# Split weights at multiples of 256 bytes, the tokens' operands 128 bytes past one

## The chip, the cores and the metric

One core of one Trainium2 chip. The metric is the device time of the whole program in microseconds: 781.03 us, the median of 3 runs (780.86, 781.03, 783.62).

## The reference, cut to what matters

One encoder layer over 512 tokens (two sequences of 256) with a model width of 1024, all in float32: an embedding LayerNorm, a token mixer, and a mixture of 16 experts of which each token takes two.

```python
z = x @ w_in + b_in                       # 1024 -> 3584: attention q, k, v; gating u, v; conv a, g
a  = neighbourhood_attention(q, k, v, rpb) @ w_a_o
bb = (gelu(u) * (W_s layer_norm(gelu(v)) + b_s)) @ w_b_o
c  = silu(layer_norm(depthwise_conv31(glu))) @ w_c_o
g  = sigmoid(x @ w_gate + b_gate)         # three gates of width 1024
m  = (g0 * a + g1 * bb + g2 * c) @ w_o + b_o
x  = layer_norm(ALPHA * x + m)
for e in range(16):                       # grouped top-2 routing
    h = silu(x @ w_e1[e]) * (x @ w_e3[e])
    y = y + gates[:, e:e + 1] * (h @ w_e2[e])
x  = layer_norm(ALPHA * x + y)
```

## The kernel before, in words

Every large product is made of float32 operands that are split in two: `hi`, the value rounded to the matmul's float32r type, and `lo`, what is left. A product is then three matmuls into one PSUM bank, hi x hi, hi x lo and lo x hi (`three`, L1841 to L1845). Each of them is one 128x128 weight load and one stream of 512 columns.

The weights come in units of 128 x 1024 float32 numbers (512 KB). SyncE's queue loads a unit into a ring of raw tiles (`raw`, in the expert stage `raw_more`, `raw_late` and `raw_rows` as well). ScalarE casts it into a slot of `w_hi` (L720), VectorE subtracts and writes a slot of `w_lo` (`cast_lo`, L1052 to L1057), and TensorE waits for `lo_cast` before it takes the unit. `w_hi` and `w_lo` have three slots of 4096 bytes per partition (`SPLIT = 3`); in the expert stage there are four (`M_SPLIT = 4`), and the fourth is in the tiles `w_hi_more` and `w_lo_more`. A slot is free again when the matmuls of its unit are done (`unit_used`).

There are two ways to use a unit. In `features` the split weights are loaded and the tokens' operands (`xT_hi`, `xT_lo`, `branch..`) stream past: so the input projections that are wanted by channel, the gates and the branch outputs. In `tokens` the tokens' operands (`xT`, `mT`, `xgT`, `hT`) are loaded and the weights stream: so v and the gating's v, the output projection and all of the experts. The profile names the operands of a matmul as moving,loaded: `bank<-xT_hi,w_hi` streams xT_hi past a load of w_hi.

The order of work is written out by hand for each engine: 28 units of input projection with attention, gating and convolution in between, 36 units of gates and branches, 8 of the output projection, the router, then 16 experts of 12 units each. For an expert the tokens' rows are gathered by an indirect DMA into `xg` (two buffers), turned by eight transposes (`turn_xg`, L2138), split into `xgT`, and multiplied; the results are scaled and scattered, and the last two experts' results are placed by matmuls with a one-hot operand (`place`, L2229 and L2230: `turned` is loaded, `placed_hi` and `placed_lo` stream) on top of an identity matmul of the running rows (L2239).

SBUF tiles are laid one behind the other in the order in which they are declared; a tile starts at the next multiple of its `line` (32 bytes, or `LINE` = 128 where that is given), and a stack that is closed gives its bytes to the tiles declared after it. The first tile, `raw`, starts at byte 16,512 of each partition. By summing the sizes: `w_hi` starts at 41,088, `w_lo` at 53,376, `const` at 65,664, `vec` at 68,192, `xT_hi` at 69,504, `mT_hi` at 152,448, `w_hi_more` at 155,520, `w_lo_more` at 159,616, `xg` at 163,712, `xgT_hi` at 171,904, `hT_hi` at 192,384. Of these `vec` is 96 bytes past a multiple of 256, and all the others are 128 bytes past one; `onehot` is at 151,040, a multiple of 256. `between` is a tile of 128 bytes that nothing reads or writes. All slots, chunks and column blocks of these operands lie at steps of 512 bytes or a multiple of that.

Of the kernel before, what the change touches and what calls it, by code (L numbers as in the profile page):

```python
# [19 lines left out]
F32R = mybir.dt.float32r  # L20
# [5 lines left out]
D = 1024  # L26
# [27 lines left out]
SPLIT = 3  # L54
M_SPLIT = 4
M_AHEAD = M_SPLIT - 1
LINE = 128
UNIT = 1024
# [10 lines left out]
V_LN1G, V_LN1B, V_ALL = 80, 88, 96  # L69
# [92 lines left out]
def encoder_layer(nc, A, out_prompt, out_sample):  # L162
    banks = plan_banks()
    ctx = ExitStack()
# [14 lines left out]
    def sb(stack, name, shape, dt=F32, line=32):  # L179
        return stack.enter_context(nc.sbuf_tensor(name, [P] + shape, dt, align_bytes=line))  # L180

    raw = sb(ctx, "raw", [RAW, UNIT])
    w_hi = sb(ctx, "w_hi", [SPLIT, UNIT], F32R)
    w_lo = sb(ctx, "w_lo", [SPLIT, UNIT], F32R)
    const = sb(ctx, "const", [C_ALL])
    vec = sb(ctx, "vec", [V_ALL])
    conv_col = sb(ctx, "conv_col", [TAPS, WC])
    stats = sb(ctx, "stats", [TT, 2, 6])
    mv = sb(ctx, "mv", [TT, 2])
# [75 lines left out]
    moe = ExitStack()  # L265
# [30 lines left out]
    gates = sb(moe, "gates", [TT, EXPERTS])  # L296
    most = sb(moe, "most", [1])
    between = sb(moe, "between", [LINE // 4])
    onehot = sb(moe, "onehot", [2, TT, SLOTS], F32R, LINE)
    joint = sb(moe, "joint", [TT, 4])  # L300
    slot_gate = sb(moe, "slot_gate", [2])
# [2 lines left out]
    list_gate = sb(moe, "list_gate", [EXPERTS])  # L304
    list_none = sb(moe, "list_none", [2, 4])
    list_base = sb(moe, "list_base", [2, 4])
    w_hi_more = sb(moe, "w_hi_more", [M_SPLIT - SPLIT, UNIT], F32R, LINE)
    w_lo_more = sb(moe, "w_lo_more", [M_SPLIT - SPLIT, UNIT], F32R, LINE)
    over_xg = ExitStack()
    xg_0 = sb(over_xg, "xg_0", [D])  # L310
    y_last_hi = sb(over_xg, "y_last_hi", [D], F32R)
    over_xg.close()
    xg = sb(moe, "xg", [2, D])
    xgT_hi = sb(moe, "xgT_hi", [2, DC, SLOTS], F32R, LINE)
# [2000 lines left out]
```

## Time and profile before

| | |
|---|---|
| median of 3 runs | 781.03 us |
| span of the profiled execution, first to last instruction | 779.0 us |
| its own time beside the span | not on the page |
| PE (matmul) busy | 747.3 us, 96% of the span, 3516 instructions |
| PEld (weight load) busy | 618.2 us, 79% |
| DVE (VectorE) busy | 609.4 us, 78% |
| ACT (ScalarE) busy | 432.6 us, 56% |
| POOL busy | 72.1 us, 9% |
| mean granted TensorE clock | 0.987 |
| DMA | 175.51 MB, mean 225 GB/s |

How to read it: PE and PEld are two views of TensorE. The duration of a matmul in the lines runs from its start to its modelled end, and matmuls overlap in the pipeline, so what a matmul takes from the span is the step from its start to the start of the next one, which the timeline shows. A row that ends in x2 or x8 merges so many instructions.

### The profile page before, as it was taken

The page shows a single profiled execution, that of the slowest core. Times are in us where ns is not written, and L with a number is a line of the kernel's source. Part 1 is how long each engine was busy: PE and PEld are TensorE (multiplying, and loading weights), DVE is VectorE, ACT ScalarE, POOL GpSimd, SP SyncE. Part 2 cuts the span into 40 slices and gives each one's busy share as a digit, 9 for nine tenths or more (in the row PEclk, how much of TensorE's full clock was granted, in tenths as well). Part 3 has the DMA queues.
Part 4 walks back from the last instruction along what each step waited for, and adds up shares of the span by engine and source line. Part 5 has one row for each costly group of instructions (what it writes and reads, how often), then busy time and mean ns, then how long its engine had stood idle before and what let it go on. Part 6 is the DMA issues. An engine that isn't in the chain of part 4 may idle for free.

```text
span 779.0 us, 10638 instructions
## 1 busy us (share of the span) xinstructions
PE 747.3 (96%) x3516; PEld 618.2 (79%) x3516; DVE 609.4 (78%) x827; ACT 432.6 (56%) x585; POOL 72.1 (9%) x96
## 2 busy tenths in 40 slices
PE   4999999999999999999999979999999999999995
PEld 3888877887888888888888857888888888888873
DVE  5799977776668866535357888999999999999977
ACT  5522134658322244623332366888888888888861
POOL 5000000000000000000011111111111111110314
PEclk9999999999999999999999989999999999999998
DMA  9734657232344352333379587999999999999882
GB/s 294 238 96 101 203 148 209 59 108 82 109 119 124 109 162 82 109 101 89 106 257 343 189 296 234 353 382 384 386 373 386 386 390 368 373 377 367 236 176 111
DMA packets 137488, 175.51 MB, mean 225 GB/s; under 512 B 15418, under 2 KB 75558, under 8 KB 137430
## 3 DMA queue, kind: packets, MB, share of 16 engines
q1 hardware_dynamic: 128896, 154.95, 59.3%
q0 software_dynamic: 7616, 19.34, 8.4%
q10 hardware_dynamic: 934, 0.69, 0.3%
q8 instruction: 23, 0.38, 0.2%
q14 instruction: 19, 0.16, 0.1%
HBM read 164.06 MB, written 19.11 MB: 235 GB/s over the span
## 4 chain that ended last, share of the span: by engine, by line
PE 85%; DVE 7%; DMA 3%; ACT 2%; SPq 2%; issue 1%; POOL 0%; DVEq 0%; ACTq 0%; POOLq 0%
PE bank L1843 25%; PE bank L1844 25%; PE bank L1845 25%; DMA raw<-in_w_in_dram 2%; PE bank L2138 2%; SPq L607 2%; DVE w_lo L1056 1%; DVE conv L1126 1%; PE bank L2059 1%; PE bank L1838 1%; PE bank L2153 1%; PE bank L2239 1%; DVE conv_odd L1126 1%; PE bank L1889 1%; PE bank L1905 1%
## 5 line engine op out<-in xcount | busy, mean ns | idle before, releaser
L1056 DVE TENSOR_TENSOR w_lo<-raw,w_hi 128x1024 fp32r<-128x1024 f32 x103 | 125.0, 1220 | 79.0 <-ACT w_hi L720 78.8
L720 ACT CAST w_hi<-raw 128x1024 fp32r<-128x1024 f32 x103 | 107.1, 1049 | 103.2 <-PE bank L1845 98.4
L1843 PE MATMUL bank<-xT_hi,w_hi 128*128 128x512 f32 x352 | 139.6, 397 | 2.9 <-DVE xT_lo L1094 1.8
L1844 PE MATMUL bank<-xT_lo,w_hi 128*128 128x512 f32 x352 | 138.2, 392 | 0.0
L1845 PE MATMUL bank<-xT_hi,w_lo 128*128 128x512 f32 x352 | 138.1, 392 | 0.0
L1843 PE MATMUL bank<-w_hi,xgT_hi 128*128 128x512 f32 x198 | 80.1, 404 | 1.0 <-issue 1.0
L1843 PEld LDWEIGHTS bank<-xT_hi,w_hi 128*128 128x128 f32 x352 | 66.8, 190 | 17.1 <-issue 3.5
L1845 PEld LDWEIGHTS bank<-xT_hi,w_lo 128*128 128x128 f32 x352 | 66.8, 190 | 14.3
L1844 PEld LDWEIGHTS bank<-xT_lo,w_hi 128*128 128x128 f32 x352 | 66.9, 190 | 13.5
L1845 PE MATMUL bank<-w_hi,xgT_lo 128*128 128x512 f32 x198 | 77.5, 391 | 0.0
L1844 PE MATMUL bank<-w_lo,xgT_hi 128*128 128x512 f32 x198 | 77.3, 390 | 0.0
L835 ACT ACTIVATE gate<-bank,vec 128x512 f32<-128x512 f32 x24 | 16.5, 688 | 83.2 <-PE bank L1845 83.2
L1056 DVE TENSOR_TENSOR w_lo<-raw_more,w_hi 128x1024 fp32r<-128x1024 f32 x40 | 48.2, 1221 | 5.7 <-ACT w_hi L720 5.4
L1056 DVE TENSOR_TENSOR w_lo<-raw_late,w_hi 128x1024 fp32r<-128x1024 f32 x40 | 48.2, 1221 | 4.0 <-ACT w_hi L720 3.9
L1126 DVE SCALAR_TENSOR_TENSOR conv<-conv_in,conv_col,conv 128x512 f32<-128x512 f32 x60 | 44.6, 744 | 0.0
L720 ACT CAST w_hi<-raw_more 128x1024 fp32r<-128x1024 f32 x40 | 41.2, 1049 | 4.5 <-PE bank L1845 4.5
L1845 PEld LDWEIGHTS bank<-w_hi,xgT_lo 128*128 128x128 f32 x198 | 37.2, 188 | 7.9
L1843 PEld LDWEIGHTS bank<-w_hi,xgT_hi 128*128 128x128 f32 x198 | 37.3, 188 | 7.8 <-issue 1.2
L720 ACT CAST w_hi<-raw_late 128x1024 fp32r<-128x1024 f32 x40 | 41.2, 1051 | 2.4 <-PE bank L1845 2.4
L1844 PEld LDWEIGHTS bank<-w_lo,xgT_hi 128*128 128x128 f32 x198 | 37.3, 188 | 6.6
L1126 DVE SCALAR_TENSOR_TENSOR conv_odd<-conv_in,conv_col,conv_odd 128x512 f32<-128x512 f32 x56 | 41.6, 743 | 0.0
L1056 DVE TENSOR_TENSOR w_lo<-raw_rows,w_hi 128x1024 fp32r<-128x1024 f32 x32 | 38.3, 1218 | 0.0
(289 smaller groups left out, 1529.3 us busy)
## 6 DMA issues: line engine op xcount, KB each, us to landing
raw_more<-in_w_e_dram SPq DMA_DIRECT2D x48, 512.0 KB, 8.4
raw<-in_w_e_dram SPq DMA_DIRECT2D x48, 512.0 KB, 9.0
raw_late<-in_w_e_dram SPq DMA_DIRECT2D x48, 512.0 KB, 8.4
raw_rows<-in_w_e_dram SPq DMA_DIRECT2D x48, 512.0 KB, 9.5
raw<-in_w_in_dram SPq DMA_DIRECT2D x28, 512.0 KB, 6.6
raw<-in_w_gate_dram SPq DMA_DIRECT2D x24, 512.0 KB, 3.7
y_scratch<-zeros SPq DMA_DIRECT2D x8, 512.0 KB, 5.1
raw<-in_w_o_dram SPq DMA_DIRECT2D x8, 512.0 KB, 3.7
```

Source lines behind the costliest of these rows:

```text
L607: sp.dma_start(v_win[:, seq, j, :], v_grid[:, WINDOW[j]:WINDOW[j] + KCOLS, :]).then_inc(v_windows, 16)
L720: act.copy(hi_slot(j), raw_slot(j)).then_inc(hi_cast, 1)
L835: act.activation(gate[:, n if n < 2 else r % 2, d, :], bank(name)[:], ACT.Sigmoid, bias=column(V_GATE + n * DC + 2 * r + d)).then_inc(free ...
L1056: dve.tensor_tensor(lo_slot(j), raw_slot(j), hi_slot(j).bitcast(F32), ALU.subtract).then_inc(lo_cast, 1)
L1126: o = dve.scalar_tensor_tensor(out=sum_, in0=shifted, scalar=conv_col[:, k, c:c + 1], in1=sum_, op0=ALU.mult, op1=ALU.add)
L1838: o = pe.transpose(bank(name)[:, k * P:(k + 1) * P], tile(k), ident)
L1843: pe.matmul(out, hi_l, hi_r, start=start, stop=False)
L1844: pe.matmul(out, hi_l, lo_r, start=False, stop=False)
L1845: return pe.matmul(out, lo_l, hi_r, start=False, stop=stop)
L1889: o = pe.matmul(bank(("attended", g))[:, j * P:(j + 1) * P], v_win[:, seq, j, hp * P:(hp + 1) * P], probsT[:, j * P:(j + 1) * P], start=Tr ...
L1905: o = pe.transpose(bank(name)[:, tokens_of(t)], x_in[:, t, c * P:(c + 1) * P], ident)
L2138: o = pe.transpose(psum[M_XT + half][:, k * P:(k + 1) * P], xg[:, q, c * P:(c + 1) * P], ident)
```

## The change

Three tiles are declared elsewhere and one gets a line. `vec` (384 bytes) is declared ahead of `w_hi` rather than behind `const`. So `w_hi` starts at 41,472 and `w_lo` at 53,760, both multiples of 256, and `const` at 66,048, a multiple of 256 as well; `conv_col` and everything behind it up to the expert stage keep their bytes. `w_hi_more` and `w_lo_more` are declared behind `between` rather than behind `list_base`: they start at 151,040 and 155,136, multiples of 256. `onehot` and the lists move up by 8,192 bytes. `xg` starts at 163,680, 96 past a multiple of 256, and `y_last_hi`, which shares its bytes, asks for a line of 128 and keeps its place at 167,808. `xgT` and all behind it keep their bytes. No instruction, wait or DMA is added, removed or put elsewhere.

```diff
@@ -180,10 +180,10 @@
         return stack.enter_context(nc.sbuf_tensor(name, [P] + shape, dt, align_bytes=line))
 
     raw = sb(ctx, "raw", [RAW, UNIT])
+    vec = sb(ctx, "vec", [V_ALL])
     w_hi = sb(ctx, "w_hi", [SPLIT, UNIT], F32R)
     w_lo = sb(ctx, "w_lo", [SPLIT, UNIT], F32R)
     const = sb(ctx, "const", [C_ALL])
-    vec = sb(ctx, "vec", [V_ALL])
     conv_col = sb(ctx, "conv_col", [TAPS, WC])
     stats = sb(ctx, "stats", [TT, 2, 6])
     mv = sb(ctx, "mv", [TT, 2])
@@ -296,6 +296,8 @@
     gates = sb(moe, "gates", [TT, EXPERTS])
     most = sb(moe, "most", [1])
     between = sb(moe, "between", [LINE // 4])
+    w_hi_more = sb(moe, "w_hi_more", [M_SPLIT - SPLIT, UNIT], F32R, LINE)
+    w_lo_more = sb(moe, "w_lo_more", [M_SPLIT - SPLIT, UNIT], F32R, LINE)
     onehot = sb(moe, "onehot", [2, TT, SLOTS], F32R, LINE)
     joint = sb(moe, "joint", [TT, 4])
     slot_gate = sb(moe, "slot_gate", [2])
@@ -304,11 +306,9 @@
     list_gate = sb(moe, "list_gate", [EXPERTS])
     list_none = sb(moe, "list_none", [2, 4])
     list_base = sb(moe, "list_base", [2, 4])
-    w_hi_more = sb(moe, "w_hi_more", [M_SPLIT - SPLIT, UNIT], F32R, LINE)
-    w_lo_more = sb(moe, "w_lo_more", [M_SPLIT - SPLIT, UNIT], F32R, LINE)
     over_xg = ExitStack()
     xg_0 = sb(over_xg, "xg_0", [D])
-    y_last_hi = sb(over_xg, "y_last_hi", [D], F32R)
+    y_last_hi = sb(over_xg, "y_last_hi", [D], F32R, LINE)
     over_xg.close()
     xg = sb(moe, "xg", [2, D])
     xgT_hi = sb(moe, "xgT_hi", [2, DC, SLOTS], F32R, LINE)
```

## Rows read from the trace of the kernel before

**Rows 1.** The page's chain that ended last: by engine, then by line.

```profile
PE 85%; DVE 7%; DMA 3%; ACT 2%; SPq 2%; issue 1%; POOL 0%; DVEq 0%; ACTq 0%; POOLq 0%
PE bank L1843 25%; PE bank L1844 25%; PE bank L1845 25%; DMA raw<-in_w_in_dram 2%; PE bank L2138 2%; SPq L607 2%; DVE w_lo L1056 1%; DVE conv L1126 1%; PE bank L2059 1%; PE bank L1838 1%; PE bank L2153 1%; PE bank L2239 1%; DVE conv_odd L1126 1%; PE bank L1889 1%; PE bank L1905 1%
```

**Rows 2.** Busy time by stretch: PE, PEld, DVE, ACT, POOL, clock, DMA share, GB/s.

```profile
300.00:430.00 130.00, 130.00 (x576) 107.57 (x575) 71.28 (x81) 45.12 (x55) 6.21 (x11) 1.00 0.48 157
...
480.00:750.00 270.00, 270.00 (x1286) 224.94 (x1285) 253.23 (x264) 231.43 (x274) 36.30 (x38) 1.00 1.01 359
```

**Rows 3.** Groups by line and shape, whole span: moving,loaded operand; busy us, mean ns.

```profile
L1844 PE MATMUL bank<-xT_lo,w_hi 128*128 128x512 f32 x352 | 138.2, 392 | 0.0
...
L1844 PE MATMUL bank<-w_lo,xgT_hi 128*128 128x512 f32 x198 | 77.3, 390 | 0.0
...
L1844 PE MATMUL bank<-branch_lo,w_hi 128*128 128x512 f32 x96 | 37.4, 389 | 0.0
...
L1844 PE MATMUL bank<-w_lo,hT_hi 128*128 128x512 f32 x90 | 35.0, 389 | 0.0
...
L1844 PE MATMUL bank<-w_lo_more,xgT_hi 128*128 128x512 f32 x66 | 25.7, 389 | 0.0
...
L1844 PE MATMUL bank<-w_lo,mT_hi 128*128 128x512 f32 x64 | 24.9, 389 | 0.0
...
L1844 PE MATMUL bank<-w_lo,xT_hi 128*128 128x512 f32 x64 | 24.9, 389 | 0.0
...
L1844 PE MATMUL bank<-w_lo_more,hT_hi 128*128 128x512 f32 x30 | 11.7, 389 | 0.0
```

**Rows 4.** Timeline of PE, mixer, weights loaded: start us, us, form.

```profile
319.79 0.39 PE L1844 MATMUL bank<-xT_lo,w_hi 128*128 128x512 f32 x1
...
323.87 0.39 PE L1844 MATMUL bank<-xT_lo,w_hi 128*128 128x512 f32 x1
```

**Rows 5.** Timeline of PE, mixer, weights streaming.

```profile
99.66 0.39 PE L1845 MATMUL bank<-w_hi,xT_lo 128*128 128x512 f32 x1
...
103.97 0.39 PE L1843 MATMUL bank<-w_hi,xT_hi 128*128 128x512 f32 x1
```

**Rows 6.** Groups by line and shape: the identity matmuls of the last sum.

```profile
L2239 PE MATMUL bank<-x,const 128*128 128x512 f32 x16 | 8.2, 591 | 0.0
```

**Rows 7.** Timeline of PE in the last sum.

```profile
758.20 0.39 PE L2230 MATMUL bank<-y_next_lo,next_turned 128*128 128x512 f32 x1
758.43 0.39 PE L2229 MATMUL bank<-y_last_hi,onehot 128*128 128x512 f32 x1
...
759.35 1.02 PE L2239 MATMUL bank<-x,const 128*128 128x512 f32 x2
```

**Rows 8.** Timeline of PE behind two f32 matmuls.

```profile
278.72 0.40 PE L1844 MATMUL bank<-branch_lo,w_hi 128*128 128x512 f32 x1
...
280.57 0.39 PE L1843 MATMUL bank<-branch_hi,w_hi 128*128 128x512 f32 x1
...
281.93 0.39 PE L1843 MATMUL bank<-branch_hi,w_hi 128*128 128x512 f32 x1
```

**Rows 9.** Groups by line and shape: three kinds of transposes.

```profile
L2138 PE MATMUL bank<-const,xg 128*128 128x128 f32 x128 | 16.6, 272 | 0.0
...
L2200 PE MATMUL bank<-const,onehot 128*128 128x128 f32 x8 | 1.2, 272 | 0.0
...
L1838 PE MATMUL bank<-const,w_s_in 128*128 128x128 f32 x4 | 0.6, 272 | 0.0
```

**Rows 10.** Groups by line and shape, 505 to 680 us: the casts on VectorE.

```profile
L1056 DVE TENSOR_TENSOR w_lo<-raw_rows,w_hi 128x1024 fp32r<-128x1024 f32 x20 | 24.0, 1218 | 0.0
...
L1056 DVE TENSOR_TENSOR w_lo_more<-raw,w_hi_more 128x1024 fp32r<-128x1024 f32 x10 | 12.4, 1239 | 1.4 <-ACT w_hi_more L720 1.4
```

**Rows 11.** Chain of waits, 64 to 125 us: start us, us, what.

```profile
68.55 1.13 DVE w_lo L1056
...
106.71 14.31 DMA raw<-in_w_in_dram
```

## The prediction

> **What bounds the kernel now.** I read the chain that ended last first. TensorE holds 85% of it, and the three matmul lines of the split product, L1843 to L1845, hold 25% of the span each [rows 1]. Then the stretches: in the dense part of the mixer (300 to 430 us) and in the expert stage (480 to 750 us) PE is busy for the whole stretch at a granted clock of 1.00, that is 2.4 GHz [rows 2]. In the expert stage VectorE is close behind, 253.23 us busy of 270.00, so 16.8 us are free there, and the DMA share reads 1.01. Nothing but the time from one matmul to the next can move this kernel much, so the question is what a start address does to that time.
>
> How many of these matmuls there are: the eight forms of L1844 count 352 + 198 + 96 + 90 + 66 + 64 + 64 + 30 = 960 [rows 3], and each belongs to a set of three, so 2,880 matmuls of 512 columns, each with a weight load of its own. In 448 of the 960 sets the split weights are loaded and the tokens stream past (the first operand named streams: xT and branch rows); in 512 sets the tokens are loaded and the weights stream (mT, xgT and hT rows, and xT with 64).
>
> Their pace: in a run with weights loaded, 18 steps take 323.87 - 319.79 = 4.08 us, 0.2267 us each [rows 4]; in a run with weights streaming, 19 steps take 103.97 - 99.66 = 4.31 us, 0.2268 us each [rows 5]. The durations of about 390 ns in the lines are pipelined and don't count; the steps do. 2,880 x 0.2267 = 653 us of the 779.0 us.
>
> **The change part by part.** No instruction, wait, semaphore, DMA or queue position is added, removed or moved. Only addresses change. Summing the declared sizes from the first tile's byte 16,512 (64 x 256 + 128): before, all four split weight tiles, xT, the branches, mT, xgT and hT start 128 bytes past a multiple of 256. After, vec's 384 bytes stand ahead of w_hi, so w_hi and w_lo start at 41,472 and 53,760, multiples of 256; the extra slots of the expert stage, w_hi_more and w_lo_more, move to 151,040 and 155,136, multiples of 256 too. The tokens' operands keep their bytes. Side effects: const moves from 128 past to a multiple of 256, onehot by 8,192 bytes, and xg from 128 past to 96 past a multiple of 256.
>
> *Term 1, the 2,880 steps.* Steps between a load and a stream that both sit 128 past are those of rows 4 and 5: 0.2267 us. Is there anything to win or lose in them? The identity matmul of L2239 streams 512 columns in plain f32: two of them take 1.02 us together and one alone about 0.59, so the second starts 0.43 us after the first; that is two passes of 512 columns, 0.214 us a pass, with a load beside it [rows 6 and 7]. A split step is longer by about 0.0127 us. So something of a load beside a full-rate stream costs 12.7 ns, and an address might matter to it. That is the most that can be won.
>
> The trace also has the pair that the change makes: in L2229 and L2230 y_last (128 past) streams while onehot (a multiple of 256) is loaded. From 758.20 to 759.35 there are five steps in 1.15 us, 0.230 us each [rows 7]. So weights loaded from a multiple of 256 against a stream 128 past give no shorter step; they are 3.3 ns longer than the steady pace. But this is just behind f32 matmuls, and there the all-128 pair is slow too: after the f32 matmuls at 278 us, eight steps take 280.57 - 278.72 = 1.85 us, 0.231 us each, and only then do six steps take 281.93 - 280.57 = 1.36 us, 0.2267 us each [rows 8]. Five steps are too few to see where the other pair would settle. The bounds of term 1 are therefore -12.7 ns and +3.3 ns a step, and I take 0: the row nearest in kind (0.230) is no slower than its own transient would be with the old offsets (0.231), and a pace that settles at the same 0.2267 for loaded and for streamed weights, and for slots 0 to 2 and slot 3 alike, doesn't look as if it hung on one distance between addresses.
>
> The Trainium skill (TensorE: Matmul & The Clock Gate, Step-by-step: what each phase is for) says that TensorE has two independent read ports, one for the streaming operand and one for the weight load. By that rule the distance between the two addresses is worth nothing and the time stays; the 12.7 ns over an f32 pass speak against so clean a picture, so I give "no change" no more than half.
>
> *Term 2, the transposes.* xg is loaded for 128 transposes. Transposes that load from 64 past (w_s_in), from 128 past (xg) and from a multiple of 256 (onehot) read 272 ns each [rows 9]. For 96 past there is no row; I take 0, and a nanosecond either way would be 0.13 us. The gather into xg is also at another offset now, but PE has no idle time in 480 to 750 us [rows 2], so it has cover; if that were gone, its delay would stop PE once per expert.
>
> *Term 3, the casts.* VectorE reads raw and w_hi and writes w_lo. Over the existing placements one cast takes from 1218 to 1239 ns [rows 10]. Were all at the long end, an expert's 12 casts would take 12 x 0.021 = 0.25 us more, and the VectorE has about 1.1 us free in each expert (16.8 us over some 15). It is hidden; only a cast of over 1.3 us would show. ScalarE's cast goes with it. vec and const as small operands: nothing.
>
> Sum: 0 + 0 + 0 on a span of 779.0 us. The page shows no total for the profiled execution; the runs' median is 781.03, so some 2.0 us lie around the span, and I forecast 781.0.
>
> **The rivals.**
> *A, slower: the new distance breaks the settled pace.* In place of 0.2267 the steps stay at the 0.230 that the onehot pair shows. Between about 64 and 122 us the mixer waits for conv work, casts and loads rather than for PE [rows 11], some 58 / 0.2267 = 256 steps, so 2,624 steps count: 2,624 x 3.3 ns = 8.7 us, 789.7. If it holds only where weights are loaded (1,344 steps), 1,344 x 3.3 = 4.4 us, 785.4. For it: the five steps of rows 7, which come four times, once for each token tile of the last sum. Against it: they follow f32 matmuls. It decides, with its sign, from 1.5 ns a step (3.9 us over 2,624 steps).
> *B, faster in part: the load and the stream stop meeting in some places.* A step shorter by the same 3.3 ns would give 781.0 - 8.7 = 772.3. For it: a part of the 12.7 ns need not be fixed. Against it: the new pair's mean in rows 7 is not below 0.2267.
> *C, faster in full: the whole 12.7 ns go.* 2,624 x 12.7 ns = 33 us, 748. In the expert stage 384 sets, 1,152 steps, would win 14.6 us, just within VectorE's free 16.8 us, so the casts would become the bound there, with the DMAs beside them. Against it: rows 7 again, plainly, though only for loaded weights; a stream from a multiple of 256 against a load 128 past has no row. The Trainium skill (TensorE: Matmul & The Clock Gate, Back-to-back issue gap) gives N/2.4 + 2.5 ns for a matmul alone, 216 ns at 512 columns; by that the gain would be 10.9 ns a step, an estimate of some 29 us.
> *D, the change does not do what it says:* the loads only sweep the same places in another order, which is the forecast itself.
>
> **How the numbers follow.** No change 0.49, A 0.29, B 0.14, C 0.08. The likeliest gives 781.0. A measurement of this kernel tells some 0.5% from no change, 3.9 us. A lies beyond that in both its forms, B and C too, so faster 0.22, same 0.49, slower 0.29. The likeliest case by itself runs from 779 to 784 (the three runs shown go to 783.62). The range for 8 in 10 takes in A with a little over it and B: 772 to 791, and leaves out C and the far ends of A and B.
>
> **What would show it.** Right: in the profile after, the steps of the runs at 320 and 100 us stay at 0.2267 us, the transient behind f32 matmuls may have other numbers, PE stays fully busy from 480 to 750 us, and the transposes of xg stay at 272 ns. A: steady steps of 0.229 to 0.232, in the weights-loaded runs at least. B and C: steady steps below 0.225; for C, VectorE's share in the expert stage near 100%. Wrong in term 2: PE idle before L2138, or transposes longer than 272 ns. Wrong in term 3: casts beyond 1.3 us and PE waiting for w_lo in the expert stage. What makes the prediction wrong above all is a steady step that differs from 0.2267 by more than 1.5 ns.

## The result: 792.6 us, slower by 1.4%

The changed kernel takes 792.6 us (median of 4 runs, 791.8 to 793.1) against 781.0 us for the kernel before. The ratio is 1.0137, with a 95% interval of 1.0115 to 1.0159. The span grew from 779.0 to 791.2 us, with the same 10,638 instructions, 3,516 of them matmuls. The mean granted clock is 0.991, against 0.987 before.

**The chain of the page after**, by engine and then by line, answers to [rows 1]:

```profile
PE 91%; DVE 4%; ACT 2%; DMA 1%; issue 1%; POOL 0%; SPq 0%; ACTq 0%; DVEq 0%
PE bank L1843 28%; PE bank L1845 27%; PE bank L1844 27%; PE bank L2138 2%; PE bank L2059 1%; DMA x_in<-in_x_sample_dram 1%; PE bank L1838 1%; PE bank L2153 1%; PE bank L2239 1%; PE bank L1889 1%; DVE w_lo L1056 1%; PE bank L2098 1%; PE bank L1879 1%; ACT probs L772 1%; ACT w_hi L720 0%
```

TensorE's share rose from 85% to 91%, all of it in the three lines of the split product. No other engine's share rose. **The stretches after** answer to [rows 2] (busy time of PE, PEld, DVE, ACT and POOL, then granted clock, DMA share, GB/s; the expert stage lies 6 us later than before):

```profile
300.00:430.00 130.00, 130.00 (x561) 105.40 (x560) 69.55 (x80) 45.58 (x56) 6.21 (x11) 1.00 0.47 154
486.00:756.00 270.00, 270.00 (x1261) 221.25 (x1260) 248.08 (x257) 226.73 (x269) 34.95 (x36) 1.00 1.00 355
```

PE is busy for the whole of both stretches at a clock of 1.00, as before, yet it gets fewer matmuls done: 561 in place of 576 (2.6% fewer), and 1,261 in place of 1,286 (1.9% fewer, transposes and all). VectorE and the DMAs did less in the same time, since they had to follow. So each matmul occupies TensorE for longer.

**The steps after.** First weights loaded and tokens streaming, the answer to [rows 4] (timeline: start in us, duration in us, form):

```profile
320.89 0.40 PE L1843 MATMUL bank<-xT_hi,w_hi 128*128 128x512 f32 x1
...
325.77 0.40 PE L1843 MATMUL bank<-xT_hi,w_hi 128*128 128x512 f32 x1
```

That is 21 steps in 4.88 us, 0.2324 us each. And tokens loaded, weights streaming, the answer to [rows 5]:

```profile
99.77 0.39 PE L1845 MATMUL bank<-w_hi,xT_lo 128*128 128x512 f32 x1
...
104.20 0.40 PE L1843 MATMUL bank<-w_hi,xT_hi 128*128 128x512 f32 x1
```

19 steps in 4.43 us, 0.2332 us each. Over the whole trace, taking every two split matmuls that follow each other directly (under 260 ns apart) and the nanosecond starts of the records, the mean step went from 227.0 to 232.45 ns with weights loaded (1,302 and 1,306 steps), and from 227.2 to 232.6 ns with weights streaming (1,460 steps each). These two means are called loaded and streaming below.

The form of the sequence changed as well. In the kernel before, a disturbance (transposes, an f32 matmul) is followed by up to some ten uneven steps (229, 233, 236, 224, 231, 236, 228 ns ...), and then every step is 226 or 227: the pace has settled, at 226.67 ns. In the kernel after it never becomes even: most of the time seven steps of 228, 230, 233, 241, 232, 231 and 232 ns go round, in other places 229 and 238 alternate.

**Behind f32 matmuls**, the answer to [rows 8]:

```profile
281.23 0.39 PE L1844 MATMUL bank<-branch_lo,w_hi 128*128 128x512 f32 x1
...
283.09 0.39 PE L1843 MATMUL bank<-branch_hi,w_hi 128*128 128x512 f32 x1
...
284.49 0.39 PE L1843 MATMUL bank<-branch_hi,w_hi 128*128 128x512 f32 x1
```

The first eight steps take 1.86 us, 0.2325 each, much as before (0.231). The next six take 1.40 us, 0.233 each, where before they took 0.2267. Only the settling is gone.

**The sum.** 1,306 x 5.44 ns is 7.1 us and 1,460 x 5.37 ns is 7.8 us: 14.9 us lost, of which the span shows 12.2. Some 3 us came back in the attention stage, for two reasons of which only the first is shown to be an effect of the change. PE's waits between 120 us and about 193 us became shorter (first the kernel before, then the kernel after; columns: what PE's line waited for, us in total, times, longest):

```profile
PE bank L1838 <- DVE probs L1163: 1.9, 1, 1.9
PE bank L1889 <- DVE branch_lo L1170: 1.8, 1, 1.8
```

```profile
PE bank L1889 <- DVE branch_lo L1170: 1.6, 1, 1.6
PE bank L1838 <- DVE probs L1163: 0.6, 1, 0.6
```

That is 3.7 us of waiting against 2.2: where VectorE ended last, a slower TensorE had less to wait for. The runs below agree: the two waits sum to 3.2 to 3.4 us in the kernels that settle at 226.67 ns (e1, e5, e11, e12) and to 2.2 in e2. The second reason is the clock behind the second wait, which differs between the two profiled executions. The stretch 185 to 201 us, before and then after:

```profile
185.00:201.00 16.00, 14.18 (x73) 12.04 (x72) 8.38 (x14) 9.08 (x16) 0.00 (x0) 0.89 0.22 66
```

```profile
185.00:201.00 16.00, 14.38 (x77) 12.08 (x76) 9.43 (x16) 10.21 (x22) 0.00 (x0) 1.00 0.32 97
```

Before, the granted clock fell to its lower level of 1.2 GHz behind an idle PE of 1.82 us, and six split steps took about 0.43 us each. After, behind 1.62 us, it stayed at 2.4 GHz. The stretch from the start of L1889 to the end of the eighth step of split matmuls took 4.86 us before (191.14 to 196.00) and 3.29 after (193.27 to 196.56), 1.6 us less. That the shorter wait kept the clock up is not shown: in e1, e5, e11 and e12 PE is idle for 1.80 to 1.81 us at the same place, and the granted clock stays at 1.00 there all the same. In e1 from 185 to 260 us, 1.80 us of 75 without PE, the columns as above:

```profile
185.00:260.00 75.00, 73.20 (x342) 61.10 (x341) 57.64 (x81) 27.25 (x38) 0.00 (x0) 1.00 0.41 119
```

So a wait of that length does not bring the fall by itself. The 1.6 us are put down to the one execution of the kernel before that was profiled (its other executions have no trace), and by that the two spans understate the cost of the change by about as much. 14.9 - 1.5 - 1.6 = 11.8, against 12.2; the 114 split matmuls that don't follow one another directly, and stretches at a low clock at either end, are in the rest.

### The profile page after: what moved, and what is told of

It is laid out like the page before. It is cut to its first block, busy times and chain, and to the rows that moved or that the text cites. A ratio compares the mean times of both kernels' runs of the same rounds, so it can differ in the third digit from the quotient of the medians.

```text
span 791.2 us, 10638 instructions
## 1 busy us (share of the span) xinstructions
PE 760.7 (96%) x3516; PEld 617.8 (78%) x3516; DVE 610.8 (77%) x827; ACT 432.2 (55%) x585; POOL 72.2 (9%) x96
## 4 chain that ended last, share of the span: by engine, by line
PE 91%; DVE 4%; ACT 2%; DMA 1%; issue 1%; POOL 0%; SPq 0%; ACTq 0%; DVEq 0%
PE bank L1843 28%; PE bank L1845 27%; PE bank L1844 27%; PE bank L2138 2%; PE bank L2059 1%; DMA x_in<-in_x_sample_dram 1%; PE bank L1838 1%; PE bank L2153 1%; PE bank L2239 1%; PE bank L1889 1%; DVE w_lo L1056 1%; PE bank L2098 1%; PE bank L1879 1%; ACT probs L772 1%; ACT w_hi L720 0%
## 5 line engine op out<-in xcount | busy, mean ns | idle before, releaser
L1843 PE MATMUL bank<-branch_hi,w_hi 128*128 128x512 f32 x96 | 38.7, 403 | 0.0
```

The lines of the kernel that those rows point to most:

```text
L1843: pe.matmul(out, hi_l, hi_r, start=start, stop=False)
```

## The experiments

All of them change start addresses alone, by moving small tiles about or by a few bytes of padding; instructions and their order stay (a declaration more or less shifts the line numbers by up to five). "Past" is the start address modulo 256. The kernel before is 128 past for weights and tokens, the kernel after 0 and 128. The ratios are to the kernel before on the same chip, where it took 779.2 us (e1 to e4), 780.3 (e5 to e8), 781.8 (e9, e10) and 780.6 (e11, e12), with 95% intervals. e3, e4 and e6 to e9 have two runs each. The fences show parts of each change against the kernel before; "..." stands for lines left out.

| kernel | weights past | tokens past | loaded, ns | streaming, ns | median us | ratio |
|---|---|---|---|---|---|---|
| before | 128 | 128 | 227.0 | 227.2 | 781.0 | 1 |
| after | 0 | 128 | 232.45 | 232.6 | 792.6 | 1.0137 (1.0115 to 1.0159) |
| e1 | 0 | 0 | 227.1 | 227.4 | 778.9 | 0.9998 (0.9979 to 1.0017) |
| e2 | 128 | 0 | 232.6 | 232.95 | 792.8 | 1.0167 (1.0146 to 1.0187) |
| e3 | 192 | 128 | 233.3 | 229.3 | 788.2 | 1.0110 (1.0083 to 1.0136) |
| e4 | 160 | 128 | 233.3 | 233.2 | 794.2 | 1.0187 (1.0159 to 1.0214) |
| e5 | fourth slots 0, others 128 | 128 | 227.1 | 228.6 | 781.7 | 1.0024 (1.0004 to 1.0043) |
| e6 | w_lo 0, w_hi 128 | 128 | 231.2 | 231.6 | 789.3 | 1.0115 (1.0067 to 1.0164) |
| e7 | 224 | 128 | 234.2 | 233.3 | 795.2 | 1.0190 (1.0142 to 1.0239) |
| e8 | 144 | 128 | 233.2 | 231.7 | 789.2 | 1.0114 (1.0058 to 1.0170) |
| e9 | 136 | 128 | 230.7 | 232.85 | 790.5 | 1.0107 (1.0078 to 1.0136) |
| e10 | 144 | 144 | 231.9 | 231.5 | 790.0 | 1.0092 (1.0065 to 1.0118) |
| e11 | 192 | 192 | 227.0 | 227.5 | 779.6 | 0.9983 (0.9962 to 1.0004) |
| e12 | 160 | 160 | 227.0 | 227.2 | 778.6 | 0.9981 (0.9956 to 1.0006) |

**e1: weights and tokens at multiples of 256.** The change, with the tokens' operands moved along.

```diff
     raw = sb(ctx, "raw", [RAW, UNIT])
+    vec = sb(ctx, "vec", [V_ALL])
     w_hi = sb(ctx, "w_hi", [SPLIT, UNIT], F32R)
...
+    ahead = sb(mix, "ahead", [LINE // 4])
     xT_hi = sb(mix, "xT_hi", [DC, T], F32R)
...
-    mT_hi = sb(late, "mT_hi", [DC, T], F32R, LINE)
+    mT_hi = sb(late, "mT_hi", [DC, T], F32R, 2 * LINE)
...
-    xgT_hi = sb(moe, "xgT_hi", [2, DC, SLOTS], F32R, LINE)
+    xgT_hi = sb(moe, "xgT_hi", [2, DC, SLOTS], F32R, 2 * LINE)
...
```

> Weights and tokens' operands all at multiples of 256 bytes (distance 0 between a load and a stream, as before, but 128 bytes further). Theory R (the pace hangs on the distance between the start of the weight load and the start of the stream, modulo 256 bytes): the steps settle at 0.2267 us as before, 781 us, within 0.5%. Theory A (a split weight tile at a multiple of 256 is slow in itself, wherever the tokens lie): steps of about 0.2324 us as in the changed kernel, 792 to 793 us. Theory S (xg at 96 past a multiple of 256 is what cost the time): xg is 128 past here, so 781 us, but with steps of 0.232 and shorter transposes.

Measured: 778.9 us, ratio 0.9998. The timeline with weights loaded:

```profile
317.77 0.39 PE L1843 MATMUL bank<-xT_hi,w_hi 128*128 128x512 f32 x1
...
321.85 0.39 PE L1843 MATMUL bank<-xT_hi,w_hi 128*128 128x512 f32 x1
```

18 steps in 4.08 us, 0.2267 each: the settled pace of 226.67 ns is back, though the weights and `const` still lie where the change put them. So the weights' new place by itself costs nothing, and nor does the moved `vec`. What costs is how the weights lie against the tokens.

**e2: weights where they were, tokens at multiples of 256.** The same distance as in the change, with the sides exchanged.

```diff
+    ahead = sb(mix, "ahead", [LINE // 4])
     xT_hi = sb(mix, "xT_hi", [DC, T], F32R)
...
-    mT_hi = sb(late, "mT_hi", [DC, T], F32R, LINE)
+    mT_hi = sb(late, "mT_hi", [DC, T], F32R, 2 * LINE)
...
-    xgT_hi = sb(moe, "xgT_hi", [2, DC, SLOTS], F32R, LINE)
+    xgT_hi = sb(moe, "xgT_hi", [2, DC, SLOTS], F32R, 2 * LINE)
...
```

> The changed kernel turned round: split weights 128 bytes past a multiple of 256 as before, the tokens' operands (xT, branches, mT, xgT, hT) moved to multiples of 256. Theory R: distance 128 again, no settled pace, steps of 0.230 to 0.233 us on average, 789 to 794 us. Theory A: the weights are where they were before, steps of 0.2267 us, 781 us.

Measured: 792.8 us, ratio 1.0167. The timeline with weights loaded:

```profile
319.92 0.40 PE L1844 MATMUL bank<-xT_hi,w_hi 128*128 128x512 f32 x1
...
324.11 0.39 PE L1844 MATMUL bank<-xT_hi,w_hi 128*128 128x512 f32 x1
```

18 steps in 4.19 us, 0.2328 each, with the same uneven round as in the kernel after. The loss is 13.6 us (792.8 against 779.2). With e1 this is the main result: it doesn't matter which side is at a multiple of 256, only that one is and the other is not.

**e3: weights 192 past.** The distance is 64, once ahead of the tokens (weights loaded) and once behind (weights streaming).

```diff
     raw = sb(ctx, "raw", [RAW, UNIT])
+    mv = sb(ctx, "mv", [TT, 2])
+    neg_max = sb(ctx, "neg_max", [2, 4])
     w_hi = sb(ctx, "w_hi", [SPLIT, UNIT], F32R)
...
-    between = sb(moe, "between", [LINE // 4])
+    between = sb(moe, "between", [40])
+    w_hi_more = sb(moe, "w_hi_more", [M_SPLIT - SPLIT, UNIT], F32R)
+    w_lo_more = sb(moe, "w_lo_more", [M_SPLIT - SPLIT, UNIT], F32R)
...
```

> Split weights 192 bytes past a multiple of 256, tokens 128 past: distance +64 where weights are loaded, -64 where they stream. Theory A: 0.2267 us everywhere, 781 us. Theory R: the two uses need not be alike; if only distance 0 settles, both read 0.229 to 0.234 us on average and the time is 787 to 794 us; if distances up to 64 still settle, 0.2267 us and 781 us. A mean step below 0.2267 us in either use would be a gain of its own.

Measured: 788.2 us, ratio 1.0110. The timeline, first weights streaming, then weights loaded:

```profile
99.02 0.39 PE L1843 MATMUL bank<-w_hi,xT_hi 128*128 128x512 f32 x1
...
103.14 0.39 PE L1843 MATMUL bank<-w_hi,xT_hi 128*128 128x512 f32 x1
...
319.85 0.39 PE L1843 MATMUL bank<-xT_hi,w_hi 128*128 128x512 f32 x1
...
324.05 0.39 PE L1843 MATMUL bank<-xT_hi,w_hi 128*128 128x512 f32 x1
```

18 steps take 4.12 us (0.229 each) where the weights stream and 4.20 us (0.233) where they are loaded. At a distance of 64 neither use reaches 226.67 ns, and the two differ. Where the weights are loaded this stretch is even all the same, every step 233 or 234 ns: a pace can settle and still be the longer one.

**e4: weights 160 past.** The distance is 32.

```diff
     raw = sb(ctx, "raw", [RAW, UNIT])
+    mv = sb(ctx, "mv", [TT, 2])
     w_hi = sb(ctx, "w_hi", [SPLIT, UNIT], F32R)
...
-    between = sb(moe, "between", [LINE // 4])
+    between = sb(moe, "between", [32])
...
```

> Split weights 160 bytes past a multiple of 256, tokens 128 past: distance +32 where weights are loaded, -32 where they stream. Theory A: 0.2267 us everywhere, 781 us. Theory R: between the paces of distance 0 (0.2267 us) and distance 64 if the pace changes smoothly with the distance; 0.2267 us if it settles over a band of distances; 0.230 us or more in both if only distance 0 settles. Times 781 to 794 us accordingly.

Measured: 794.2 us, ratio 1.0187, steps of 233.3 and 233.2 ns. A distance of 32 is no better than one of 128.

**e5: the fourth slots alone at multiples of 256.**

```diff
     between = sb(moe, "between", [LINE // 4])
+    w_hi_more = sb(moe, "w_hi_more", [M_SPLIT - SPLIT, UNIT], F32R, LINE)
+    w_lo_more = sb(moe, "w_lo_more", [M_SPLIT - SPLIT, UNIT], F32R, LINE)
     onehot = sb(moe, "onehot", [2, TT, SLOTS], F32R, LINE)
...
```

> One part of the change alone: w_hi_more and w_lo_more at multiples of 256 (with xg at 96 past, as in the change), w_hi and w_lo left 128 past; 288 of the 2,880 steps have distance 128. If every step pays for its own pair and nothing else: these steps read 0.2324 us, the others 0.2267, 288 x 5.7 ns = 1.6 us slower than before. If the pace is a state that one pair upsets and that settles again later: behind each of the 48 fourth-slot units some 2 to 9 steps of the other slots are long as well (0.228 to 0.236 us), about 1.4 us more, 3.0 us slower in all. If the fourth slot's pairs don't matter: same time as before.

Measured: 781.7 us, ratio 1.0024 (1.0004 to 1.0043). The timeline through one unit of the fourth slot and what follows it:

```profile
570.03 0.39 PE L1843 MATMUL bank<-w_hi_more,xgT_hi 128*128 128x512 f32 x1
...
571.42 0.39 PE L1843 MATMUL bank<-w_hi,xgT_hi 128*128 128x512 f32 x1
...
573.69 0.39 PE L1844 MATMUL bank<-w_lo,xgT_hi 128*128 128x512 f32 x1
```

By the nanosecond starts the unit's six steps take 1.383 us, 0.2305 each; the next ten, with all at 128 past, take 2.271 us, 0.2271. Over the trace the steps of fourth slots have a mean of 231.45 ns, the other streaming ones 227.9. So the cost belongs to the matmuls whose own two operands lie apart, plus a few steps until the pace settles. Being a part of the change, it costs a part: 1,460 x (228.6 - 227.2) = 2.0 us by the steps, and 0.24% of 780.3 us is 1.9 us. That lies between the 1.6 and 3.0 us of the two expectations.

**e6: only the lo weights at multiples of 256.** One load or stream in three is apart from its partner.

```diff
     w_hi = sb(ctx, "w_hi", [SPLIT, UNIT], F32R)
+    vec = sb(ctx, "vec", [V_ALL])
     w_lo = sb(ctx, "w_lo", [SPLIT, UNIT], F32R)
...
+    w_lo_more = sb(moe, "w_lo_more", [M_SPLIT - SPLIT, UNIT], F32R, 2 * LINE)
...
```

> w_lo and w_lo_more at multiples of 256, w_hi and w_hi_more 128 past, tokens 128 past: one load in three (or one stream in three) has distance 128. If every step pays for its own pair: one step in three at 0.2324 us, mean 0.2286 us, 2,880 x 1.9 ns = 5.5 us slower, some 784.6 us against 779.2. If one pair in three keeps the pace from settling at all: mean 0.231 to 0.233 us in all three lines, 12 to 14 us slower, as the whole change.

Measured: 789.3 us, ratio 1.0115. The timeline with weights loaded:

```profile
318.18 0.39 PE L1842 MATMUL bank<-xT_hi,w_hi 128*128 128x512 f32 x1
...
322.33 0.39 PE L1842 MATMUL bank<-xT_hi,w_hi 128*128 128x512 f32 x1
```

18 steps in 4.16 us by the nanosecond starts, 0.2311 each. With the tokens' part named first, the steps that start with hi x hi, lo x hi and hi x lo are 227.1, 232.4 and 234.0 ns where weights are loaded, and 232.3, 229.6 and 232.7 where they stream. The odd matmul is hi x lo, behind lo x hi where weights are loaded and behind hi x hi where they stream: the step into it and the step out of it are long, and the third is shorter. So one odd matmul in three lengthens the step ahead of it too, and three quarters or more of the cost remains (4.2 of 5.4 ns, and 4.4 of 5.4). Neither expectation fits: the loss is 9.0 us (789.3 against 780.3), between 5.5 and 12 to 14, and not all three lines are long.

**e7, e8 and e9: weights 224, 144 and 136 past.** Distances of 96, 16 and 8. The last two are not at multiples of 32 either.

```diff
     raw = sb(ctx, "raw", [RAW, UNIT])
+    mv = sb(ctx, "mv", [TT, 2])
+    neg_max = sb(ctx, "neg_max", [2, 4])
+    exp_sum = sb(ctx, "exp_sum", [2, 4])
     w_hi = sb(ctx, "w_hi", [SPLIT, UNIT], F32R)
...
```

> Split weights 224 bytes past a multiple of 256, tokens 128 past: distance +96 where weights are loaded, -96 where they stream. From the distances seen (0: 0.2267 both ways; +32 0.2333 loaded, -32 0.2332 streaming; +64 0.2333 loaded, -64 0.2292 streaming; 128 0.2325): means between 0.229 and 0.234 us in both uses, 787 to 794 us. A theory in which the loss grows evenly up to 128 would have wanted 0.228 us at 32 and is already out; one in which -64 is the edge of a good band would give 0.2292 us or less for -96.

```diff
-    w_hi = sb(ctx, "w_hi", [SPLIT, UNIT], F32R)
-    w_lo = sb(ctx, "w_lo", [SPLIT, UNIT], F32R)
+    ahead = sb(ctx, "ahead", [4])
+    w_hi = sb(ctx, "w_hi", [SPLIT, UNIT], F32R, 16)
+    w_lo = sb(ctx, "w_lo", [SPLIT, UNIT], F32R, 16)
...
```

> Split weights 144 bytes past a multiple of 256, tokens 128 past: distance +16 where weights are loaded, -16 where they stream. If only an exact match settles: 0.229 to 0.234 us, 787 to 794 us. If what counts is a block of 32 bytes or more: 0.2267 us, 779 to 781 us. A mean below 0.2267 us would point to a better placement than the kernel before has.

```diff
-    w_hi = sb(ctx, "w_hi", [SPLIT, UNIT], F32R)
-    w_lo = sb(ctx, "w_lo", [SPLIT, UNIT], F32R)
+    ahead = sb(ctx, "ahead", [2])
+    w_hi = sb(ctx, "w_hi", [SPLIT, UNIT], F32R, 8)
+    w_lo = sb(ctx, "w_lo", [SPLIT, UNIT], F32R, 8)
...
```

> Split weights 136 bytes past a multiple of 256, tokens 128 past: distance +8 where weights are loaded, -8 where they stream. If the two starts have to match to the element: 0.230 to 0.234 us, 787 to 794 us. If they have to match to a block of 16 bytes or so (the distances of 16 and more all failed): 0.2267 us in the steps of one or both uses, 779 to 782 us.

Measured: 795.2, 789.2 and 790.5 us, ratios 1.0190, 1.0114 and 1.0107, steps between 230.7 and 234.2 ns. None reaches 226.67, and e7 is a little over the 794 us and 0.234 us that were expected at most. The size of the cost doesn't grow with the distance: 32 bytes (e4) cost 6.3 ns (loaded) and 6.0 ns (streaming), 128 bytes 5.4. In e8 and e9 two things differ at once, the distance and the multiple of 32, and e10 shows that the second is enough by itself; so they say nothing on distances of 16 and 8.

**e10: weights and tokens both 144 past.** The distance is zero, as before, but the starts are no multiples of 32.

```diff
+    ahead = sb(ctx, "ahead", [4])
+    w_hi = sb(ctx, "w_hi", [SPLIT, UNIT], F32R, 16)
+    w_lo = sb(ctx, "w_lo", [SPLIT, UNIT], F32R, 16)
...
+    lead_x = sb(mix, "lead_x", [4])
+    xT_hi = sb(mix, "xT_hi", [DC, T], F32R, 16)
+    xT_lo = sb(mix, "xT_lo", [DC, T], F32R, 16)
...
```

> Split weights and all tokens' operands 144 bytes past a multiple of 256: distance 0, but no operand at a multiple of 32. Theory R (only the distance counts): the steps settle at 0.2267 us, the same time as before within 0.5%, where weights at 144 against tokens at 128 gave 0.2332 and 0.2317 us. A theory that a start at a multiple of 128 is good in itself, and that 144 was slow for being none: 0.230 us or more, 787 us or more.

Measured: 790.0 us, ratio 1.0092. The timeline, weights streaming and weights loaded:

```profile
98.70 0.39 PE L1848 MATMUL bank<-w_hi,xT_hi 128*128 128x512 f32 x1
...
102.86 0.39 PE L1848 MATMUL bank<-w_hi,xT_hi 128*128 128x512 f32 x1
...
319.44 0.40 PE L1848 MATMUL bank<-xT_hi,w_hi 128*128 128x512 f32 x1
...
323.64 0.40 PE L1848 MATMUL bank<-xT_hi,w_hi 128*128 128x512 f32 x1
```

18 steps take 4.16 us (0.231) and 4.20 us (0.233). The steps are even, 230 to 232 ns in the first stretch and 233 or 234 in the second, but the pace of 226.67 isn't reached. So the theory that the distance alone decides falls: among starts at multiples of 32 no unequal pair reached 226.67 (the kernel after, e2, e3, e4, e7), but equal starts are not enough.

**e11 and e12: both 192 past, and both 160 past.** The distance is zero and the starts are multiples of 64 and of 32.

```diff
+    mv = sb(ctx, "mv", [TT, 2])
+    neg_max = sb(ctx, "neg_max", [2, 4])
     w_hi = sb(ctx, "w_hi", [SPLIT, UNIT], F32R)
...
+    lead_x = sb(mix, "lead_x", [16])
     xT_hi = sb(mix, "xT_hi", [DC, T], F32R)
...
```

> Weights and all tokens' operands start 192 bytes past a multiple of 256: the distance is zero and the start is a multiple of 64, not of 128. If equal starts need only be at a multiple of 64 (or 32): steps of 0.2267 us, settled, as in the kernel before, time 779 to 782 us. If they must be at a multiple of 128: steps of 0.230 to 0.234 us that don't settle, as with both at 144, time 787 to 795 us.

```diff
+    mv = sb(ctx, "mv", [TT, 2])
     w_hi = sb(ctx, "w_hi", [SPLIT, UNIT], F32R)
...
+    lead_x = sb(mix, "lead_x", [8])
     xT_hi = sb(mix, "xT_hi", [DC, T], F32R)
...
```

> Weights and all tokens' operands start 160 bytes past a multiple of 256: distance zero, start a multiple of 32, not of 64. If a multiple of 32 is enough: steps of 0.2267 us, time 779 to 782 us. If 64 or 128 is needed: steps of 0.230 to 0.234 us, time 787 to 795 us. The two of this call together place the limit: both settled, 32 suffices; only the one at 192, 64 is needed; neither, 128 (or another rule).

Measured: 779.6 and 778.6 us, ratios 0.9983 (0.9962 to 1.0004) and 0.9981 (0.9956 to 1.0006). The timeline of e11 with weights streaming, and of e12 with weights loaded:

```profile
98.36 0.39 PE L1847 MATMUL bank<-w_hi,xT_hi 128*128 128x512 f32 x1
...
102.44 0.39 PE L1847 MATMUL bank<-w_hi,xT_hi 128*128 128x512 f32 x1
```

```profile
318.20 0.39 PE L1847 MATMUL bank<-xT_hi,w_hi 128*128 128x512 f32 x1
...
322.28 0.39 PE L1847 MATMUL bank<-xT_hi,w_hi 128*128 128x512 f32 x1
```

4.08 us for 18 steps in both, 0.2267 each. So of equal starts 0, 128, 160 and 192 past settle at 226.67 and 144 doesn't: a multiple of 32 is enough. That it is needed rests on the one start of 144. e4 against e12 is the cleanest pair of all: the same weights, the tokens moved by 32 bytes, 1.0187 against 0.9981.

## Why the prediction was wrong

*What bounds the kernel*: right. TensorE is busy in both dense stretches, before and after, and only the step from one matmul to the next could move the time.

*Term 1, the 2,880 steps*: this failed. I had taken 0 for the new distance, within -12.7 and +3.3 ns; it is +5.4 ns. The trace had a row of the new pair: the five steps in which `y_last` (128 past) streams past a load of `onehot` (a multiple of 256) took 0.230 us [rows 7]; the first of the five starts with `y_next_lo` past `next_turned`, both 128 past. I set it aside because the transient behind f32 matmuls is as slow [rows 8], and that comparison was sound: these five steps could not tell the two apart. The error was the next step, the argument that a pace which is the same for loaded and for streamed weights, and for all slots, doesn't look as if it hung on one distance. Every one of those cases had its two operands at the same place modulo 256, so they could say nothing on another one. Of the odd pair nothing in the trace showed a settled pace, and I gave it the settled pace of the other pair. The same five steps after:

```profile
770.40 0.39 PE L2230 MATMUL bank<-y_next_lo,next_turned 128*128 128x512 f32 x1
770.63 0.40 PE L2229 MATMUL bank<-y_last_hi,onehot 128*128 128x512 f32 x1
...
771.57 1.02 PE L2239 MATMUL bank<-x,const 128*128 128x512 f32 x2
```

Here `onehot` was moved by 8,192 bytes, so the pair is the same modulo 256. By the nanosecond starts of the records the five steps take 1.165 us, 0.2330 each, where the same pair took 1.149, 0.2298 each, in the kernel before. Five steps behind f32 matmuls are thus not the settled price even of their own pair: the upper bound of 3.3 ns was a reading of a transient.

*Rival A* named the mechanism and its sign, with a chance of 0.29, and gave 789.7 us. Two of its sizes were off. The price of a step was 5.4 ns and not 3.3. And 2,624 steps were too few, since no steps between 64 and 122 us should have been left out. I had read rows of casts and DMAs in the chain there [rows 11] as a stretch that doesn't wait for PE. After the change the chain through the same stretch, by line, is:

```profile
by line: PE bank L1843 30.2%; PE bank L1845 29.9%; PE bank L1844 29.8%; DVE conv L1126 3.2%; DVE conv_odd L1126 2.2%; DVE w_lo L1056 2.0%; ACT w_hi L720 1.7%; DVE vs L1218 1.2%; issue 0.4%; ACTq L719 0.0%
```

90% of it is the split product. In the kernel before, too, PE had only one wait from 64 to 125 us:

```profile
PE bank L1843 <- DVE vs L1218: 1.0, 1, 1.0
```

The first split matmul behind those of the scores (L1879) came 2.8 us later than before (128.59 against 125.76 us), and 2.5 of these arose after 31 us, about what 414 steps of 5.4 ns make (94 us by 0.2267). A chain can pass through other engines while TensorE, working without a gap beside it, is as late as they are. Against these stand the 3.1 us that came back, which no term had; as far as the traces show, 1.6 of them hang on the clock of one execution and are luck. The range up to 791 ended where A's own price ended, with little for its uncertainty; the time lies 1.6 us beyond it.

*Rivals B and C*, a shorter step, are refuted for every placement that was run: no kernel had a mean under 227.0 ns. The 12.7 ns over an f32 pass are not for an address of these to win; that an f32 matmul of 512 columns is two passes is a reading of its 428 ns, which no run tests.

The Trainium skill (TensorE: Matmul & The Clock Gate, Step-by-step: what each phase is for) speaks of two independent read ports for stream and load. Taken for the time of a step, that would give one time for all placements of this table; the runs differ from the kernel before by up to 1.9%, so for the time of a step the two are not independent here.

*Term 2, the transposes*, held. The transposes of `xg`, 96 past now, by line after (duration in ns as minimum, median and maximum, first and last start), then the identity matmuls and the other transposes by form, the answer to [rows 6, 9]:

```profile
L2138 PE MATMUL bank<-const,xg x128: 270/273/476, 475.8 to 741.0; 128*128 128x128 f32 x128
```

```profile
L2239 PE MATMUL bank<-x,const 128*128 128x512 f32 x16 | 8.2, 591 | 0.0
...
L2200 PE MATMUL bank<-const,onehot 128*128 128x128 f32 x8 | 1.2, 272 | 0.0
...
L1838 PE MATMUL bank<-const,w_s_in 128*128 128x128 f32 x4 | 0.6, 271 | 0.0
```

The median is 273 ns against 272 (means 277 and 272). The long ones lie at 476 us, where the granted clock was at its lower level until 476.7 us; in the kernel before it had risen at 468.8 us, ahead of the first of these transposes at 469.4. *Term 3, the casts*, held as well. VectorE, the answer to [rows 10], from 511 to 692 us:

```profile
L1056 DVE TENSOR_TENSOR w_lo<-raw_rows,w_hi 128x1024 fp32r<-128x1024 f32 x20 | 24.0, 1219 | 0.1
...
L1056 DVE TENSOR_TENSOR w_lo_more<-raw,w_hi_more 128x1024 fp32r<-128x1024 f32 x10 | 12.4, 1240 | 1.7 <-ACT w_hi_more L720 1.7
```

1219 and 1240 ns against 1218 and 1239. Both tiles moved by 128 bytes or more, and VectorE doesn't notice.

**What stays open.** Why the pace of 226.67 ns is reached for equal starts alone is not shown: no record tells what a load or a stream waits for inside a step. By the records a weight load is as long before as after (median 188 ns), and what grows is the time from its end to the next matmul's start, from 36 to 41 ns (medians). The runs give the condition and its price only. Whether the padding of e10 acts through the loads or through the streams wasn't separated, and no distance beyond those of the table was run.

## What to carry to other kernels

Where a kernel is bound by full-rate matmuls that each load new weights, keep the loaded and the streaming operand at the same start modulo 256, and that at a multiple of 32; moving one side alone, even by 32 bytes, cost 1 to 2% here, and it is found in the mean step between matmuls and in no busy share. Before a pace is taken to be independent of something, look whether the rows ever vary it. A price read from five steps behind a disturbance needs a wide range: the same five read 0.2298 and 0.2330 us in two kernels.

## What the runs showed of the hardware

- The settled step of a 512-column split matmul with a load of its own is 226.67 ns at 2.4 GHz, in every kernel with equal starts at multiples of 32. Where all weights and tokens lie otherwise the means are 229.3 to 234.2 ns, in some stretches even (233 or 234 throughout in e3 and e10, weights loaded) and in others not. No placement beat the one of the kernel before.
- Modulo 512 is too fine. In the kernel before `w_hi` is 128 past a multiple of 512 and `xT_hi` and `xgT_hi` 384, while `w_hi_more` and `xgT_hi` are both 384 past: a distance of 256 bytes settles at 226.67 just as a distance of 0 does, and one of 128 doesn't.
- The cost is not symmetrical. A load 64 bytes past its stream takes 233.3 ns a step, a load 64 bytes short of it 229.3 (e3); the two also differ in which operand is at 128 and which at 192.
- Pairs of matmuls in plain f32 don't show it between before and after: the identity matmuls of L2239 start 428 or 429 ns apart in the kernel before, where `x` (128 past) streams past a `const` at 128, and in the kernel after, where `const` is at a multiple of 256. In e10, with `const` at 144, they start 428 to 434 apart.
